# Expert weights in paired, fixed ring slots: gate/up pieces of 4 MB with 32 KB rows for 27 of 32 experts, and a loop over pairs of experts on TensorE

## The reference, cut to what matters

```python
def expert_block(args):
    xb, e = args
    gu = xb @ w_gate_up[e] + b_gate_up[e]
    gate, up = gu[:, :D_EXPERT], gu[:, D_EXPERT:]
    gate = jnp.minimum(gate, SWIGLU_LIMIT)
    up = jnp.clip(up, -SWIGLU_LIMIT, SWIGLU_LIMIT)
    act = (up + 1.0) * gate * jax.nn.sigmoid(SWIGLU_ALPHA * gate)
    return act @ w_down[e] + b_down[e]
```

## Time and profile before

| | |
|---|---|
| median of 3 runs | 1264.06 us (1262.4 to 1265.34) |
| the profiled execution | 1263.88 us, its span 1262.1 us |
| mean granted clock of TensorE | 0.993 of 2.4 GHz |
| TensorE busy | 1162.4 us, 92% |
| read from HBM | 443.40 MB, 352 GB/s over the span |
| SyncE waiting for TensorE at L311 / L316 | 382.7 / 163.2 us |
| TensorE's weight loads waiting for gate/up chunks | 106.4 us in 61 waits |

### The profile page before, as it was taken

One profiled execution on the slowest core, in us unless ns is written; L12 is line 12 of the kernel. 1 busy time (PEld: TensorE's weight loads), 2 busy tenths in 40 slices (PEclk: granted clock), 3 DMA queues, 4 the chain that ended last, 5 costly groups with the idle time before them and its releaser, 6 DMA issues.

```text
span 1262.1 us, 16197 instructions
## 1 busy us (share of the span) xinstructions
PE 1162.4 (92%) x6670; PEld 567.8 (45%) x6670; DVE 268.7 (21%) x626; ACT 173.3 (14%) x284; POOL 28.0 (2%) x60
## 2 busy tenths in 40 slices
PE   8999999999799999999998888888888888888885
PEld 5955875875544444444443333333333333333332
DVE  4334455113612111121111111111111111111112
ACT  3222111023301110011100000010110010000001
POOL 3000010010200000000000000000000000000000
PEclk9999999999899999999999999999999999999999
DMA  8933300576799999999999999999999999999993
GB/s 262 365 133 133 133 10 1 210 257 241 274 419 426 429 427 427 428 427 428 426 428 427 428 428 426 428 427 427 428 428 427 427 427 427 427 429 427 427 427 138
DMA packets 53055, 445.42 MB, mean 353 GB/s; under 512 B 8896, under 2 KB 9312, under 8 KB 28192
## 3 DMA queue, kind: packets, MB, share of 16 engines
q1 hardware_dynamic: 52560, 442.87, 84.6%
q0 software_dynamic: 432, 1.59, 0.5%
HBM read 443.40 MB, written 1.05 MB: 352 GB/s over the span
## 4 chain that ended last, share of the span: by engine, by line
PE 58%; DMA 38%; issue 2%; DVE 2%; ACT 0%; SPq 0%; DVEq 0%
PE bank L730 26%; DMA ring<-in_w_gate_up 19%; DMA slot<-in_w_gate_up 19%; PE bank L504 12%; PE bank L495 7%; PE bank L740 3%; PE bank L754 3%; PE bank L515 2%; PE bank L474 1%; PE bank L805 1%; DMA ring<-in_w_in 1%; PE bank L797 1%; PE bank L617 1%; PE bank L668 1%; PE bank L649 1%
## 5 line engine op out<-in xcount | busy, mean ns | idle before, releaser
L730 PE MATMUL bank<-ring,region 128*64 128x512 f32 x1696 | 381.0, 596 | 41.7 <-DMA ring<-in_w_gate_up 28.3
L730 PE MATMUL bank<-slot,region 128*64 128x512 f32 x1376 | 309.9, 595 | 36.0 <-DMA slot<-in_w_gate_up 25.6
L730 PEld LDWEIGHTS bank<-ring,region 128*64 128x64 f32 x1696 | 133.7, 137 | 264.2 <-issue 207.2
L730 PEld LDWEIGHTS bank<-slot,region 128*64 128x64 f32 x1376 | 107.6, 137 | 218.2 <-issue 165.7
L1360 DVE TENSOR_SCALAR region<-bank 128x512 f32<-128x512 f32 x32 | 22.1, 691 | 713.3 <-PE bank L730 713.3
L504 PE MATMUL bank<-ring,slot 128*128 128x512 f32 x352 | 153.5, 594 | 0.1
L829 ACT ACTIVATE region<-bank 128x512 f32<-128x512 f32 (+2 forms) x136 | 72.8, 544 | 344.4 <-PE bank L730 231.2
L504 PEld LDWEIGHTS bank<-ring,slot 128*128 128x128 f32 x352 | 66.3, 190 | 79.9 <-issue 78.9
L829 ACT ACTIVATE bank<-region 128x512 f32<-128x512 f32 x32 | 19.3, 602 | 498.7 <-DVE region L1360 498.7
L495 PE MATMUL bank<-slot,ring 128*128 128x256 f32 x384 | 84.2, 380 | 0.0
L495 PEld LDWEIGHTS bank<-slot,ring 128*128 128x128 f32 x384 | 72.6, 190 | 10.4 <-issue 0.5
(11 more groups left out here) (181 smaller groups left out, 493.8 us busy)
## 6 DMA issues: line engine op xcount, KB each, us to landing
ring<-in_w_gate_up SPq DMA_DIRECT2D x70, 2048.0 KB, 46.4
slot<-in_w_gate_up SPq DMA_DIRECT2D x58, 2048.0 KB, 47.9
ring<-in_w_down SPq DMA_DIRECT2D x36, 2048.0 KB, 47.8
slot<-in_w_down SPq DMA_DIRECT2D x27, 2048.0 KB, 47.6
ring<-in_w_in SPq DMA_DIRECT2D x7, 2048.0 KB, 19.4
ring<-in_w_xkv SPq DMA_DIRECT2D x4, 2048.0 KB, 8.0
ring<-in_w_out SPq DMA_DIRECT2D x2, 2048.0 KB, 7.6
ring<-in_w_xq SPq DMA_DIRECT2D x2, 2048.0 KB, 7.8
```

Of the source, the lines that this page charges most:

```text
L730: last = pe.matmul(bk[half * ROWS:(half + 1) * ROWS, :], lhs, w[:, half * 512:(half + 1) * 512], start=start, stop=stop, skip_group_check= ...
```

## The change

All 11 places become slots of one tile `ring`. The slot of a chunk no longer goes round 11 places: chunks 0 to 10 and (1,5) stay where n mod 11 has them, and from expert 2 on a pattern of 12 chunks repeats for each pair of experts. Gate/up of an even expert goes to slots 1 to 4, gate/up of an odd one to 7 to 10, and down of both to 5 and 6. Slot 0 takes (1,5) and then only (31,4). SyncE still issues in the order of the numbers, and each load waits for the use of the chunk that last had its slot.

For experts 4 to 30 two gate/up chunks come in one transfer of 4 MB, in which a partition gets four neighbouring rows of `w_gate_up`, 32 KB together; TensorE waits once for both. Experts 0 to 3 and 31 keep single chunks, each of which is half of such rows (16 KB out of 32 KB). The gather's columns therefore have a step of 4 instead of 2. TensorE's program has experts 0 to 3 and 30, 31 in straight code, and experts 4 to 29 as a loop of 13 rounds over two experts, with the slots fixed and the semaphore counts in registers. SyncE reads the table before each load.

```diff
@@ -63,10 +63,14 @@
 GU_CHUNKS = 4
 DOWN_CHUNKS = 2
 CHUNKS = GU_CHUNKS + DOWN_CHUNKS
-GU_ROWS = KT // GU_CHUNKS
+ROWS_PER = 4
+WIDE = 2
 DOWN_ROWS = KT // DOWN_CHUNKS
-LOADS = CHUNKS * E
+GU_TILES = KT // GU_CHUNKS
 RING = 11
+HALVED = 4
+PAIRS = (E - HALVED) // 2 - 1
+SLOT = 4096
 MAXW = MAXB * E
...
-        ring = sb("ring", SLOTS * 4096)
-        slot6, slot7, slot8, slot9, slot10 = (sb(f"slot{k}", 4096) for k in range(6, 11))
-        region5, region6 = slot6[:, 0:2048], slot6[:, 2048:4096]
-        region1, region2 = slot7[:, 0:2048], slot7[:, 2048:4096]
-        x_res_t, region10 = slot8[:, 0:2048], slot8[:, 2048:4096]
-        s_t, row_t = slot9[:, 0:3072], slot9[:, 3072:4096]
-        region3, tmp_t, late = slot10[:, 0:2048], slot10[:, 2048:3072], slot10[:, 3072:4096]
+        ring = sb("ring", RING * SLOT)
+
+        def part(slot, first, last):
+            return ring[:, slot * SLOT + first:slot * SLOT + last]
+
+        panel_slots = (3, 1, 2, 6, 7, 0)
+        region5, region6 = part(4, 0, 2048), part(4, 2048, 4096)
+        s_t, row_t = part(5, 0, 3072), part(5, 3072, 4096)
+        region1, region2 = part(8, 0, 2048), part(8, 2048, 4096)
+        x_res_t, region10 = part(9, 0, 2048), part(9, 2048, 4096)
+        region3, tmp_t, late = part(10, 0, 2048), part(10, 2048, 3072), part(10, 3072, 4096)
...
         def panel(n):
-            s = n % SLOTS
-            return ring[:, s * 4096:(s + 1) * 4096].rearrange("p (k n) -> p k n", n=PW)
-
-        places = [ring[:, s * 4096:(s + 1) * 4096] for s in (5, 1, 2, 0)] + [slot6[:, :], slot9[:, :]]
-        places += [ring[:, s * 4096:(s + 1) * 4096] for s in (3, 4)] + [slot7[:, :], slot8[:, :], slot10[:, :]]
-        out_tile = tm(slot9, 0)
+            return part(panel_slots[n % SLOTS], 0, SLOT).rearrange("p (k n) -> p k n", n=PW)
+        def slot_of(e, k):
+            n = e * CHUNKS + k
+            if n <= RING:
+                return n % RING
+            if (e, k) == (E - 1, CHUNKS - 2):
+                return 0
+            j = n % (2 * CHUNKS)
+            return j + 1 if j < RING - 1 else j - 5
+        order = [(e, k) for e in range(E) for k in range(CHUNKS)]
+        wide = [(e, k) for e in range(HALVED, E - 1) for k in range(0, GU_CHUNKS, WIDE)]
+        second_halves = [(e, k + 1) for e, k in wide]
+        held_by = [[c for c in order if slot_of(*c) == s] for s in range(RING)]
+        loads_of = [[c for c in held if c not in second_halves] for held in held_by]
+        def nth_load(e, k):
+            return loads_of[slot_of(e, k)].index((e, k)) + 1
+        def used_before(e, k):
+            held = held_by[slot_of(e, k)]
+            return held[held.index((e, k)) - 1]
+        out_tile = tm(part(1, 0, SLOT), 0)
...
-            def load_chunk(n):
-
-                e, k = n // CHUNKS, n % CHUNKS
-                dst, arrived = places[n % RING], chunk_in[n % RING]
+            def load_wide(e, k):
+                rows, s = ROWS_PER * P, slot_of(e, k)
+                src = A["w_gate_up"][0, e, k // 2 * rows:(k // 2 + 1) * rows, :].rearrange("(p a) n -> p (a n)", a=ROWS_PER)
+                sp.dma_start(part(s, 0, WIDE * SLOT), src).then_inc(chunk_in[s], 16)
+            def load_chunk(e, k):
+                arrived = chunk_in[slot_of(e, k)]
+                dst = part(slot_of(e, k), 0, SLOT)
                 if k < GU_CHUNKS:
-                    rows = GU_ROWS * P
-                    src = A["w_gate_up"][0, e, k * rows:(k + 1) * rows, :].rearrange("(p a) n -> p (a n)", a=GU_ROWS)
+                    rows, c0 = ROWS_PER * P, k % 2 * SLOT
+                    src = A["w_gate_up"][0, e, k // 2 * rows:(k // 2 + 1) * rows, :].rearrange("(p a) n -> p (a n)", a=ROWS_PER)
+                    sp.dma_start(dst, src[:, c0:c0 + SLOT]).then_inc(arrived, 16)
+                    return
+                rows, r0 = DOWN_ROWS * P, (k - GU_CHUNKS) * DOWN_ROWS * P
+                src = A["w_down"][0, e, r0:r0 + rows, :].rearrange("(p a) n -> p (a n)", a=DOWN_ROWS)
+                if (e, k) != order[-1]:
                     sp.dma_start(dst, src).then_inc(arrived, 16)
                     return
-                rows = DOWN_ROWS * P
-                src = A["w_down"][0, e, (k - GU_CHUNKS) * rows:(k - GU_CHUNKS + 1) * rows, :].rearrange("(p a) n -> p (a n)", a=DOWN_ROWS)
-                if n < LOADS - 1:
-                    sp.dma_start(dst, src).then_inc(arrived, 16)
-                    return
-                half = DOWN_ROWS * D // 2
+                half = SLOT // 2
                 sp.dma_start(dst[:, 0:half], src[:, 0:half]).then_inc(arrived, 16)
-                sp.dma_start(dst[:, half:2 * half], src[:, half:2 * half]).then_inc(last_half_in, 16)
+                sp.dma_start(dst[:, half:SLOT], src[:, half:SLOT]).then_inc(last_half_in, 16)
...
-            load_chunk(10)
-
-            for n in range(RING, LOADS):
-                before, k = (n - RING) // CHUNKS, (n - RING) % CHUNKS
-                if k == 0 or n == RING:
-                    used = sp.value_load(table[0:1, before + 2 * E + 1:before + 2 * E + 2], min_val=0, max_val=CHUNKS * MAXW)
-                sp.wait_ge(sem["chunk_used"], sp.snap(used + (k + 1)))
-                load_chunk(n)
+            load_chunk(1, 4)
+            for e, k in order[RING:]:
+                if (e, k) in second_halves:
+                    continue
+                before, kb = used_before(e, k + 1 if (e, k) in wide else k)
+                used = sp.value_load(table[0:1, before + 2 * E + 1:before + 2 * E + 2], min_val=0, max_val=CHUNKS * MAXW)
+                sp.wait_ge(sem["chunk_used"], sp.snap(used + (kb + 1)))
+                if (e, k) in wide:
+                    load_wide(e, k)
+                else:
+                    load_chunk(e, k)
...
-                for c in range(GU_CHUNKS):
-                    for a in range(GU_ROWS):
-                        k = c * GU_ROWS + a
-                        first = c * GU_ROWS * P + a
-                        for i in range(3):
-                            for t in range(NT):
-                                last = pe.matmul(bank_a[:, k * ROWS:(k + 1) * ROWS],
-                                                 h2_parts[:, i, t, first:first + GU_ROWS * P - a:GU_ROWS], sel[:, t, :],
-                                                 start=(i == 0 and t == 0), stop=(i == 2 and t == NT - 1), skip_group_check=True)
+                for k in range(KT):
+                    c, a = k // ROWS_PER * ROWS_PER * P, k % ROWS_PER
+                    for i in range(3):
+                        for t in range(NT):
+                            last = pe.matmul(bank_a[:, k * ROWS:(k + 1) * ROWS],
+                                             h2_parts[:, i, t, c + a:c + ROWS_PER * P:ROWS_PER], sel[:, t, :],
+                                             start=(i == 0 and t == 0), stop=(i == 2 and t == NT - 1), skip_group_check=True)
                 last.then_inc(sem["xb_psum"], 1)
-            def chunk_of(e, k):
-                n = e * CHUNKS + k
-                return places[n % RING], chunk_in[n % RING], 16 * (n // RING + 1)
...
-            for e in range(E):
-                blocks = pe.value_load(table[0:1, e:e + 1], min_val=1, max_val=MAXB)
-                first = pe.value_load(table[0:1, e + E:e + E + 1], min_val=0, max_val=MAXW)
+            def expert(e, slots, counts, final=False):
+
+                blocks = pe.value_load(table[0:1, bass.ds(e, 1)], min_val=1, max_val=MAXB)
+                first = pe.value_load(table[0:1, bass.ds(e + E, 1)], min_val=0, max_val=MAXW)
                 with pe.Fori(0, blocks) as c:
...
-                        wk, arrived_k, count = chunk_of(e, k)
-                        pe.wait_ge(arrived_k, count)
-                        for a in range(GU_ROWS):
-                            f = k * GU_ROWS + a
+                        wk = part(slots[k], 0, SLOT)
+                        if counts[k] is not None:
+                            pe.wait_ge(chunk_in[slots[k]], counts[k])
+                        for a in range(GU_TILES):
+                            f = k * GU_TILES + a
...
-                        wk, arrived_k, count = chunk_of(e, GU_CHUNKS + j)
-                        pe.wait_ge(arrived_k, count)
+                        wk = part(slots[GU_CHUNKS + j], 0, SLOT)
+                        pe.wait_ge(chunk_in[slots[GU_CHUNKS + j]], counts[GU_CHUNKS + j])
                         for a in range(DOWN_ROWS):
-                            if e == E - 1 and j == DOWN_CHUNKS - 1 and a == DOWN_ROWS // 2:
+                            f = DOWN_ROWS * j + a
+                            if final and f == KT - DOWN_ROWS // 2:
                                 pe.wait_ge(last_half_in, 16)
-                            f = DOWN_ROWS * j + a
...
+            def slots(e):
+                return [slot_of(e, k) for k in range(CHUNKS)]
+            def counts(e):
```

(35 more changed lines are left out.)

## The result

The changed kernel takes 1271.7 us (median of 4 runs, 1270.51 to 1274.28) against 1263.23 us for the kernel before (median of 4). The ratio is 1.0068, with a 95% interval of 1.0045 to 1.0091. The profiled execution took 1270.75 us, 6.9 us more than that of before.

The account below looks back on a forecast made before the run. Taking transfers as the bound from 347 us on, it summed 1263.88 us + 16.5 (gap) - 4.0 (packets) - 2.0 (code) = 1274.4 us, slower by 0.8%, with a range of 1266 to 1284 us.

Parts of the forecast that it names:

- What bounds it: From 347 us on transfers set the time; an idle DMA microsecond costs one at the end, TensorE has 3.4 us spare.
- The gap at (3,4): Load (3,4) on SyncE's queue is issued at 416.91 us, the queue dry at 401; 16.5 us lost.
- The byte count: Gap sized from bytes moved: queue dry at 401 us, flowing again at 418.7, 17.6 us lost.
- the landings: Gap sized by when (3,4) lands: 424.4 us instead of 409.0, 15.4 us later.
- That it comes once: After (3,4) no later load starves the queue, as TensorE gains 3 us on the flow in every expert.
- the wait of (3,4) for (2,4): In slot 5, (3,4) waits for (2,4) instead of (1,5), five chunks of TensorE's work later, holding up all loads behind.
- The packets: Gate/up transfers in 32 KB rows: 6,912 packets fewer at 9.2 ns a row, 4.0 us saved.
- The code: TensorE's loop code fetched once: 26 packets of 1.1 us fewer over 16 engines, 2.0 us saved, at most 4.
- TensorE: Gather with step 4 grows by 0.54 us, taken as nothing; registers, counts and table reads fit the 3.4 us to spare.
- The fast one: Rival: 32 KB rows hold 436 GB/s at the landings, 20.4 us less, 1260 us; chance 0.10.
- The rows weren't cut up: Rival: the queue cuts rows at 16 KB, packets stay at 53,055 and the gap remains, 1278 us; chance 0.08.
- TensorE didn't become the bound: Rival: loop jumps waiting for code cost 68 us, 1342 us, or a slow gather does the like; chance 0.10.

Follow-up runs that it names:

- e5: Changed kernel with fixed slots beginning at expert 10 instead of 2, 4 MB transfers only for experts 10 to 30; 1257.38 us, 0.9959 of the kernel before.
- e4: Changed kernel with (3,4) put in the empty slot 0, so that it waits for (1,5) as before; 1270.29 us, 1.0056 of the kernel before.
- e7: As the changed kernel, but with the fixed slots beginning at expert 6 instead of expert 2; 1261.38 us, 0.9986 of the kernel before.
- e2: Changed kernel with all gate/up chunks as single 2 MB transfers in 16 KB rows, slots and loop kept; 1276.12 us, 1.0105 of the kernel before.
- e3: Changed kernel with its 4 MB transfers written in rows of 16 KB, gather step 2 again; 1276.3 us, 1.0099 of the kernel before.
- e1: Changed kernel with experts 4 to 29 in straight code instead of the loop; 1278.13 us, 1.0121 of the kernel before.
- e6: Changed kernel with fixed slots from expert 10, plus 4 MB transfers for experts 4 to 9 where slots lie side by side; 1255.66 us, 0.994 of before.

## Why the prediction was right

**What bounds it** held: 17.4 us without transfers, with TensorE busy, came back at the end, 16.5 us of it by e5.

**The gap at (3,4)** was placed right and sized well: 16.5 us predicted, 17.4 seen in the profile and 16.5 by e5. (3,4) was issued at 415.83, forecast 416.91, and the queue was dry at 400, forecast 401. The byte count (17.6) came nearer to the trace than the landings (15.4). That it comes once held too. But the prediction named the wait of (3,4) for (2,4) as the cause, and e4 shows that this is too narrow: with it gone the next down chunk pays. The step to state is that the down chunks have two slots, and that most of TensorE's lead must be gone before that is enough. e7 gives the size between.

**The packets**: 4.0 us predicted, 4.4 by e2, and the quiet pair 0.29 us shorter as worked out (58.72 to 58.43). e3 adds that it is the row, not the transfer. The forecast of about 46,140 packets had left out the 864 small ones and those of the program; the page has 45,248. The pair's 0.31 us between e2 and the changed kernel over 32 rows of one engine is 9.7 ns a row. The Trainium skill (DMA: Bandwidth & Descriptors, Measured) derives about 10.5 ns a packet from a 4 KB transfer of 64 packets. That the two lie close proves little: the page divides the time of the whole transfer by its packets, and its packets are 256 times smaller.

**The code** is the term that was mis-sized: 2.0 us predicted, 6.4 by e1's median and 5.4 by its landings. The step that failed is the division of 26 packets by 16 engines. A packet of 1.1 us doesn't cost a landing a sixteenth of that. The parts of the transfers in e1 show that seven of eight packets cost nothing, while every eighth puts one part, and with it the landing, back by 1.45 to 1.49 us. (Eight packets by the prediction's way would be 0.55 us.) The number of packets was short as well, 32 and not 26. The rows of before held this: the prediction read the mean of 29.62 us and a lag of the landings behind the flow, and gave the packets of code a bound of 4 us; it didn't look at the landings one by one. With 5.4 to 6.4 instead of 2.0 the sum would have been 1271.0 to 1270.0 us, within 0.8 us of the profiled execution. The other misses cancel: the gap was 0.9 us longer than forecast, and the stretch from the last landing to the end, which the prediction left as it was, grew by 0.9 us; in this execution the experts began 1.8 us earlier, which is chance.

**TensorE** stayed within its spare time. The gather grew from 1.40 to 1.60 us in the chain, where 0.54 us more was the bound:

```profile
L791 PE MATMUL bank<-region,r_levels 128*128 128x64 bf16 x1584 | 59.1, 199 | 1.6 <-DVE region L1392 1.5
```

Busy for 59.1 us now, it was busy for 52.8 us before. The twelve jumps cost nothing that can be seen: pairs in the loop take 58.43 us, and TensorE waits as long for the landing that has a jump before it (566.13) as for one that has none (536.93):

```profile
536.93 7.09 PE L769 MATMUL bank<-ring,region 128*64 128x512 f32 x32 [2.41 <-DMA ring<-in_w_gate_up]
566.13 8.78 PE L769 MATMUL bank<-ring,region 128*64 128x512 f32 x32 [2.40 <-DMA ring<-in_w_gate_up]
```

The rule of the Trainium skill on taken branches (Runtime: NRT & Kernel Launch, Instruction fetch mechanics) foretells a stop when the target is outside the window of fetched pages, and calls full unrolling the preferred form for that reason. Here it came out the other way: the packets of the program fell from 54 to 22, with none at all between 496 and 1223 us, so the rounds of the loop weren't fetched again, and straight code was slower by 6.4 us. Whether a loop that is too long for this would stop, no run shows.

**The rivals.** The fast one fell: landings stood 29.26 us apart and would have had to stand below 29.01. The rows weren't cut up (45,248 packets). TensorE didn't become the bound, but for the last expert, 0.9 us.

## What to carry to other kernels

Where transfers set the time, ask of each slot not only how many there are but how long after its last use its next load is wanted, at the moment when the ring is fullest. A pattern that is deep enough in the steady state can cost the whole lead that the compute engine still has when it begins; begin it later, as e5 and e6 do. Longer rows and a loop in place of straight code each won some 4 to 6 us here, and both were hidden by one gap of 17 us, so take the parts of such a change one by one. And where a small cost is spread over 16 engines, look at single landings and not at their mean.

## What the runs showed of the hardware that wasn't expected

Code costs transfers. TensorE's straight code makes every third pair of experts 1.55 us longer (before, and e1), though all packets of the program together take 0.3% of the DMA engines. One late part of 16 makes the whole landing late.

After the longer waits for 4 MB the granted clock of TensorE mostly falls to its lower level for a moment. Stretches of the changed kernel around the landing at 566.13:

```profile
560.00:562.00 2.00, 2.00 (x12) 0.74 (x10) 0.00 (x0) 0.00 (x0) 0.00 (x0) 1.00 1.10 475
562.00:566.00 4.00, 1.73 (x10) 0.30 (x4) 0.00 (x0) 0.00 (x0) 0.00 (x0) 1.00 0.89 381
566.00:568.00 2.00, 1.87 (x6) 0.66 (x8) 0.00 (x0) 0.00 (x0) 0.00 (x0) 0.56 1.02 434
568.00:570.00 2.00, 2.00 (x8) 0.52 (x6) 0.00 (x0) 0.00 (x0) 0.00 (x0) 0.59 1.04 442
```

The engine had stood idle for 2.40 us, and then its mean clock was 0.56 and 0.59 of 2.4 GHz over 4 us: about 3.4 us at the lower level, 1.2 GHz, and the rest at the upper one. The 32 matmuls took 8.78 us instead of 7.09. Of the changed kernel's 14 waits of 2.4 us or more for gate/up, 10 were followed by such a slow group (8.61 to 8.78 us) and 4 by 7.09 us; of its 11 waits of 0.7 to 1.6 us none was. With the 1.25 us waits of the kernel before and of e2 the groups of the chain kept 3.65 us. In the middle of the loop it is hidden. Where such a landing is the last of the chain, as in the profiled execution of e1 (8.71 us after 1215.33), it costs 1.6 us.
